# Another order for the first stage of a decoder-layer kernel, and in-projection chunks of 272, 384 and 392 tokens

## The reference, cut to what matters

```python
def rms_norm(x, w):
    x32 = x.astype(jnp.float32)
    y = x32 * lax.rsqrt(jnp.mean(x32 * x32, axis=-1, keepdims=True) + EPS)
    return (y * w.astype(jnp.float32)).astype(x.dtype)
...
    xn = rms_norm(h, n_mix_pre)
    proj = xn @ w_in
    q, k, v, g, a, b = jnp.split(proj, [RET_W, 2 * RET_W, 3 * RET_W, 4 * RET_W, 4 * RET_W + CONV_CH], axis=-1)
```

## Time and profile before

| | |
|---|---|
| median of 3 runs | 1182.92 us |
| the 3 runs | 1182.92, 1183.08, 1179.6 us |
| time of the profiled execution | 1179.61 us |
| its span | 1177.7 us |
| PE busy | 1148.5 us, 98% of the span |
| DVE, POOL, ACT busy | 803.7, 614.0, 445.6 us |

### The profile page before, as it was taken

The page is one execution under the profiler, slowest core; times in us unless marked ns, Lnnn a source line. Parts: engine busy times, 40 slices in busy tenths (PEclk is TensorE's granted clock), DMA queues, the critical chain, the costliest instruction groups (busy, mean ns, idle before and its releaser), DMA issues.

```text
span 1177.7 us, 22886 instructions
## 1 busy us (share of the span) xinstructions
PE 1148.5 (98%) x8651; PEld 1130.5 (96%) x8651; DVE 803.7 (68%) x1243; ACT 445.6 (38%) x798; POOL 614.0 (52%) x454
## 2 busy tenths in 40 slices
PE   7999999999999999799999999999999999999997
PEld 6999999999999987599999999999999999999997
DVE  5548899953546237988585858485958586767646
ACT  5444444323335335542333333333333333333313
POOL 3056788404112347566564747474737373737416
PEclk9999999999999999899999999999999999999999
DMA  9311111103144313212111121212121212121134
GB/s 299 111 36 48 43 54 37 54 3 100 36 130 110 119 72 139 79 37 67 43 48 60 36 70 36 71 36 71 36 71 36 71 36 71 36 70 37 55 144 163
DMA packets 102360, 84.53 MB, mean 72 GB/s; under 512 B 2722, under 2 KB 89378, under 8 KB 102298
## 3 DMA queue, kind: packets, MB, share of 16 engines
q1 hardware_dynamic: 102114, 83.61, 22.7%
q10 hardware_dynamic: 192, 0.17, 0.0%
HBM read 72.86 MB, written 11.38 MB: 72 GB/s over the span
## 4 chain that ended last, share of the span: by engine, by line
PE 90%; DVE 3%; POOL 3%; issue 2%; DMA 1%; ACT 1%; DVEq 0%; ACTq 0%; POOLq 0%
PE ps L409 28%; PE ps L411 28%; PE ps L410 28%; POOL o_last L816 1%; POOL h_ring L774 1%; DVE w_ring L1575 1%; PE ps L1765 1%; PE ps L1804 1%; PE ps L1939 1%; PE ps L1869 1%; PE ps L1888 1%; PE ps L1993 1%; PE ps L1992 1%; DMA t_sm<-table_identity_decays 1%; POOL st L611 1%
## 5 line engine op out<-in xcount | busy, mean ns | idle before, releaser
L1711 DVE TENSOR_TENSOR ffn_acc<-ps,ffn_acc 128x516 f32<-128x516 f32 x264 | 183.8, 696 | 7.9 <-PE ps L411 2.6
L409 PE MATMUL ps<-xn_hi,w_hi 128*128 128x350 f32 (+2 forms) x576 | 187.2, 325 | 0.2 <-DVE xn_lo L1280 0.2
L411 PE MATMUL ps<-xn_lo,w_hi 128*128 128x350 f32 (+2 forms) x576 | 185.2, 322 | 0.0
L410 PE MATMUL ps<-xn_hi,w_lo 128*128 128x350 f32 (+2 forms) x576 | 184.9, 321 | 0.0
L409 PE MATMUL ps<-x_hi,w_ring 128*128 128x256 f32 x616 | 174.8, 284 | 4.9 <-DVE e_s L1589 3.8
L409 PE MATMUL ps<-x,w_ring 128*128 128x260 f32 x616 | 175.4, 285 | 1.7 <-issue 1.2
L410 PE MATMUL ps<-x,w_ring 128*128 128x260 f32 x616 | 175.3, 285 | 0.0
L411 PE MATMUL ps<-x,w_ring 128*128 128x260 f32 x616 | 175.0, 284 | 0.0
L411 PE MATMUL ps<-x_lo,w_ring 128*128 128x256 f32 x616 | 174.1, 283 | 0.0
L410 PE MATMUL ps<-x_hi,w_ring 128*128 128x256 f32 x616 | 174.0, 283 | 0.0
L409 PE MATMUL ps<-act_hi,w_ring 128*128 128x258 f32 x560 | 158.2, 283 | 0.1
(11 more groups left out here) (256 smaller groups left out, 2754.4 us busy)
## 6 DMA issues: line engine op xcount, KB each, us to landing
f_raw<-in_w_ffn_in SPq DMA_DIRECT2D x42, 512.0 KB, 3.8
raw<-in_w_in SPq DMA_DIRECT2D x24, 512.0 KB, 3.7
f_raw<-in_w_ffn_out SPq DMA_DIRECT2D x22, 512.0 KB, 4.0
x_st<-in_x_prompt SPq DMA_DIRECT2D x8, 512.0 KB, 8.1
raw<-in_w_out SPq DMA_DIRECT2D x8, 512.0 KB, 6.5
h_ring<-in_x_prompt SPq DMA_DIRECT2D x8, 512.0 KB, 4.5
h_scratch<-h_ring SPq DMA_DIRECT2D x8, 512.0 KB, 3.0
h_fin<-h_scratch SPq DMA_DIRECT2D x8, 512.0 KB
```

Of the source, the lines that this page charges most:

```text
L409: nc.tensor.matmul(out, hi, mhi, start=first, stop=False, skip_group_check=resumes)
L410: nc.tensor.matmul(out, lo, mhi, start=False, stop=False, skip_group_check=resumes)
L411: return nc.tensor.matmul(out, hi, mlo, start=False, stop=last, skip_group_check=resumes)
L1711: v.tensor_tensor(a, tile_banks(i), a, ALU.add).then_inc(s_acc, 1)
```

## The change

It has four parts. The three chunks are cut at 272 and 656 tokens in place of 350 and 700. The table with the identity (`t_sm`) is loaded first on SP and no longer third on ACT. The orders of the first stage are new on ACT, DVE and PE, token tile 3 is transposed after the first half of job (0,0) and into another pair of banks, and the waits of jobs for tiles follow the new borders. And `w_lo` of unit 0 is written by POOL, between its powers of tiles 3 and 4.

```diff
-IN_CHUNKS = [(0, 350), (350, 350), (700, T_IN - 700)]
-QG_CHUNKS = [(META, 350 - META)] + IN_CHUNKS[1:]
+IN_CHUNKS = [(0, META + 2 * P), (META + 2 * P, 3 * P), (META + 5 * P, 3 * P + NS)]
+QG_CHUNKS = [(META, 2 * P)] + IN_CHUNKS[1:]
...
+        def x_pair(t):
+
+            return 1 if t == 3 else 2 + t % 2
...
+            sp.dma_start(t_sm[:, :], tab[:, :]).then_inc(s_tab, 16)
             load_x(1)
...
                 power(st[0:n, 20 + t:21 + t], st[0:n, 10 + t:11 + t], s_var, t + 1, s_rstd)
+                if t == 3:
+                    pool.wait_ge(s_whi, 1)
+                    g.tensor_tensor(w_lo[:, 0, :], raw[:, 0, :], w_hi[:, 0, :].bitcast(F32),
+                                    ALU.subtract).then_inc(s_wlo, 1)
...
-            act.dma_start(t_sm[:, :], tab[:, :]).then_inc(s_tab, 16)
...
             x_square(0)
             x_square(1)
-            for t in range(9):
+            x_square(2)
+            x_hi(0)
+            x_square(3)
+            x_hi(1)
+            w_split_hi(0)
+            x_hi(2)
+            x_square(4)
+            x_hi(3)
+            x_square(5)
+            w_split_hi(1)
+            for t in range(4, 9):
                 if t + 2 < 9:
                     x_square(t + 2)
                 x_hi(t)
-                if t in (2, 3):
-                    w_split_hi(t - 2)
...
             x_var(0)
+            x_var(1)
             dve.wait_ge(s_gpre, 16)
             x_scale(0)
-            x_var(1)
-            for t in range(1, 9):
-                if t + 1 < 9:
-                    x_var(t + 1)
-                x_scale(t)
-                if t == 4:
-                    w_split_lo(1)
+            x_scale(1)
+            x_var(2)
+            x_lo(0)
+            x_scale(2)
+            x_var(3)
+            x_lo(1)
+            x_scale(3)
+            x_lo(2)
+            x_var(4)
+            x_scale(4)
+            x_lo(3)
+            x_var(5)
+            x_scale(5)
+            dve.wait_ge(s_wlo, SLOTS + 1)
+            w_split_lo(1)
+            for t in range(4, 9):
+                if t + 2 < 9:
+                    x_var(t + 2)
+                    x_lo(t)
+                    x_scale(t + 2)
                 else:
-                    x_lo(t - 1)
-                if t == 3:
-                    w_split_lo(0)
-                    x_lo(3)
-            x_lo(8)
+                    x_lo(t)
...
-                if t >= 2:
-                    pe.wait_ge(s_xlo, t - 1)
+                if t == 2 or t >= 4:
+                    pe.wait_ge(s_xlo, {2: 1, 4: 3, 5: 2}.get(t, t - 1))
...
-            for t, n in enumerate((12, 6, 3, 16)):
+                    tr(ps[:, 1, 0:P], ident, ident)
+
+            for t, n in enumerate((24, 2, 6)):
                 keep_busy(n)
                 x_tile(t)
-            keep_busy(24)
-            for un, c, first, then, tiles in ((0, 0, 4, 5, 4), (1, 0, 6, 7, 4), (0, 1, 8, None, 7)):
+            keep_busy(16)
+            for un, c, first, then, tiles in ((0, 0, 3, 4, 3), (1, 0, 5, 6, 4), (0, 1, 7, 8, 6)):
                 first_job(un, c, tiles, 0, KT // 2)
                 x_tile(first)
                 first_job(un, c, tiles, KT // 2, KT)
-                if then is not None:
-                    x_tile(then)
+                x_tile(then)
```

More of the change, by code:

```diff
@@ L126, in build @@
         rope = at("rope", [P, 2, T_IN], B + 12 * tile_b)
-        swp = at("swp", [P, 2, 350], B + 14 * tile_b)
-        rc = at("rc", [P, 2, 350], B + 15 * tile_b)
+        swp = at("swp", [P, 2, IN_CHUNKS[2][1]], B + 14 * tile_b)
+        rc = at("rc", [P, 2, IN_CHUNKS[2][1]], B + 15 * tile_b)
         junk0 = at("junk0", [P, D], B + 15 * tile_b)
@@ L850, in x_hi @@
                 act.wait_ge(s_xT, t + 1)
-                src = ps2[:, 2 + t % 2, :].rearrange("p (k n) -> p k n", k=KT)
+                src = ps2[:, x_pair(t), :].rearrange("p (k n) -> p k n", k=KT)
                 if t == 0:
@@ L1761, in x_tile @@
                 pe.wait_ge(s_xs, t + 1)
-                if t >= 2:
-                    pe.wait_ge(s_xlo, t - 1)
+                if t == 2 or t >= 4:
+                    pe.wait_ge(s_xlo, {2: 1, 4: 3, 5: 2}.get(t, t - 1))
                 for k in range(KT):
-                    ins = tr(ps2[:, 2 + t % 2, k * P:k * P + n], xs_st[0:n, t % 3, k * P:(k + 1) * P], ident[0:n, 0:n])
+                    ins = tr(ps2[:, x_pair(t), k * P:k * P + n], xs_st[0:n, t % 3, k * P:(k + 1) * P], ident[0:n, 0:n])
                 ins.then_inc(s_xT, 1)
@@ L1803, in keep_busy @@
                 for _ in range(n):
-                    tr(ps[:, 2, 0:P], ident, ident)
-            for t, n in enumerate((12, 6, 3, 16)):
+                    tr(ps[:, 1, 0:P], ident, ident)
+            for t, n in enumerate((24, 2, 6)):
                 keep_busy(n)
                 x_tile(t)
-            keep_busy(24)
-            for un, c, first, then, tiles in ((0, 0, 4, 5, 4), (1, 0, 6, 7, 4), (0, 1, 8, None, 7)):
+            keep_busy(16)
+            for un, c, first, then, tiles in ((0, 0, 3, 4, 3), (1, 0, 5, 6, 4), (0, 1, 7, 8, 6)):
                 first_job(un, c, tiles, 0, KT // 2)
```

## The result

The changed kernel took **1186.75 us** (median of 19 runs, 1184.84 to 1189.66), the kernel before 1182.92 (19 runs on the same chip, 1179.6 to 1185.49): ratio **1.0036, 95% interval 1.0028 to 1.0043**, so 3.3 to 5.1 us slower.

A forecast was written before the change was run, and what follows sets the result against it. PE was taken to bound the kernel, busy 1148.5 of 1177.7 us. Job (1,1) later +0.8, work behind it -0.6 and one clock fall +2.0 gave +2.2 on 1182.9: 1185.1 us, range 1180.5 to 1188.5.

The forecast's parts named there:

- The start: First stage up to job (0,0): it starts at 18.8 us against 23.07, 4.3 earlier.
- The stall: Before job (1,0): PE idles 3.4 us until unit 1's `w_lo` is ready; the job starts at 27.0 us.
- The tail: Before job (1,1): PE idles 2 us behind tile 8; the job starts at 40.7 us, a shift of +0.8.
- The clock: PE's two new idle gaps in the first stage: one fall of the granted clock, costing 2.0 us (1 to 3).
- The work: Matmuls of the new chunks: 2.0 us saved over all units, 1.4 us more left behind job (1,1).
- Net behind (1,1): Matmul work after job (1,1): 1.4 us more, less 2.0 saved by the chunks, -0.6 us (-2.1 to +2.2).
- The base: Whole kernel before the change: two levels, 1179.6 and 1183 us, most runs on the upper; 1182.9 us taken.
- Rival 2: First stage: two clock falls or more, or one also slowing tiles 0 to 2; +4.2 us, 1187.1, chance 0.24.
- the one-fall case: First stage: the granted clock falls once in the new gaps; +2.2 us in all, 1185.1 us, chance 0.38.

## Why the prediction came out as it did

Point by point, in its own order.

- **The start: right.** Table at 3.40 (3.8 said), job (0,0) at 18.10 (18.8, 17.9 to 18.8), `x_scale(3)` 3.30 us long (over 3).
- **The stall: right.** PE idled 3.12 us (3.4) before job (1,0), released by DVE's `w_lo`; at full clock the distance is 8.14 us (8.25). The fall of the clock inside it makes 9.71 of that, and since it began 0.7 early, job (1,0) came at 27.81 in place of 27.0.
- **The tail: right,** 2.09 us (2).
- **The clock: the mechanism right, the count wrong, the size by chance.** One fall of 6.8 us for 2.0 was taken; there were two of 3.4 us, for 2.96 together. 40.7 + 2.0 = 42.7 was said for job (1,1) with one fall, 42.94 measured: the 0.7 us that the start came early and the 0.96 that the falls cost more nearly cancel. From job (0,0) to (1,1) at full clock it is 21.88 us, as said (21.9). Of the four waits of 3 us in the profiles three were followed by a fall, so the count is not fixed by their length.
- **The work: the failed term, by size.** "Net behind (1,1): 1.4 - 2.0 = -0.6" was +0.28, so the steady saving was 1.1 us and not 2.0. The mis-sized prices are 272 columns (0.1252, said 0.1245) and 392 (0.1783, said 0.177), both inside their bounds. The price that makes the difference is one that I took over unchanged: 384 columns cost 0.1752 in this stage, not the 0.1735 that the earlier trace rows have from the output projection. With it the three chunks come to 0.479 against 0.481, 0.0018 less and not 0.006. Over 24 units of 24 matmuls that is 1.0 us, near the 1.1 measured. I had given this price no bounds. The constant part per matmul that the page "TensorE: Matmul & The Clock Gate" of the Trainium skill gives (section "Back-to-back issue gap", for a matmul by itself), and by which the saving would be 0, is not borne out either.
- **What was not in the sum:** the half-clock time at the samples' products. It differs by 3.3 us between the two profiles and by 1.65 between two of the unchanged kernel, so it moves single profiles about as much as the whole change was said to. The shift at job (1,1), against a kernel before with (1,1) at 38.55 to 39.9, is 3.0 to 4.4 us, and with the 0.28 behind it 3.3 to 4.7, where the ratio gives 4.3 (3.3 to 5.1). So it is enough without this stretch; with 1.6 to 3.3 more from the stretch the sum would be 4.9 to 8.0. How much of the stretch stands in the medians isn't shown.
- **The base:** of the three runs I made two levels, 1179.6 and 1183. The 19 runs show one spread, from 1181.7 to 1185.5, with 1179.6 alone below it.
- **Two readings of rows.** The transposes ahead of tile 0 start 0.21 us apart, not 0.235, which is their busy time of 2.82 us by 12; and the fall in the earlier trace rows is at 488.2, not 488.4 (a PEclk of 0.60 over a microsecond is 0.8 of it at 0.50). Neither moves the sum: tile 1 waited for DVE, and the fall's length of 6.8 us is right.
- **Rival 2** (two falls, +4.2 us) is what came about, within 0.1 us of the measured difference, but by luck in the size: its two falls were half as long, and (1,1) came at 42.94, near the 42.7 of the one-fall case and not at 44.7. The rest came from the work (0.9) and from a kernel before that reaches (1,1) at times 1.2 us before the 39.78 of its first profile.

So the time went into an order that starts early and then waits. The start was won (5 us), the stall and the tail gave it back (3.1 + 2.1), and the clock took 3 on top (2.96 between job (0,0) and (1,1), in the profiled execution). The sum is rough: one tile more (0.8 us) and 1.3 us less of jobs lie between the two jobs as well. What stays open: why filling both gaps gave less in the medians than at job (1,1), what the tail costs by itself, and what sets the length of the half-clock stretch at the samples' products.

## What to carry to other kernels

Price an earlier start by the next thing that is late, in the order in which each engine issues it; here the first job came 5 us earlier, and the second needed an operand that stood 8 us behind the first. Test the parts of a change apart: the table's load first, in the old order, was worth most of a gain of 0.28%, and the new orders beside it turned that into a loss of 0.36%. Take the price of a matmul from the stage that it runs in: 1.7 ns of difference at 384 columns were 1.0 us of the sum. A gap on a dense TensorE can cost more than its length: where the clock fell behind one, that took another 1.5 us.

## What the runs showed of the chip

- The granted clock fell to 0.50 while PE was busy for every microsecond, in a run of matmuls of one column (0.109 us apart at 2.4 GHz, 0.21 at 1.2). It fell 2.3 to 5.5 us behind the first of them, in each of eleven profiles. With sixteen 128-column transposes among 64 of them it fell too, 5.2 and 6.1 us behind the first.
- The waits of the new orders, each after dense work, and the clock behind them: of four of 2.99 to 3.12 us three were followed by 3.4 us at 1.2 GHz, one of 2.24 us was not, and of five of 2.09 us two were. Each of these falls cost about 1.5 us.
- At the program's start the transposes came 0.21 us apart, and 0.11 apart from 12.0 to 12.4 us in four profiles and from 16.9 to 18.3 in the four others of the old order with the table landing at 8.8 to 9.0 in all; with the same first stage, job (1,1) came 1.2 to 1.7 us later in these. PEclk reads 1.00 in these rows all the while, so the spacing has to be read there.
- The spacing of starts lay above columns/2.4 GHz by a part that was not constant: 11.9 ns at 272 columns and 15 at 392, and at 384 columns 15 in the in-projection and 13.5 in the output projection.
